# One encoder block on one core: the border to the down projection, the adaLN sums, and who forms the lower parts of the heads' weights

## The reference, cut to what matters

```
mod = silu(c) @ w_ada + b_ada                      # 6 vectors of 2048: shift, scale, gate, twice
h = rmsnorm(x, g_norm1) * (1 + sc1) + sh1
x = x + gt1 * hybrid_mixer(h)                      # mLSTM heads and windowed attention
h = rmsnorm(x, g_norm2) * (1 + sc2) + sh2
x = x + gt2 * ((silu(h @ w_gate) * (h @ w_up)) @ w_down)   # w_down: 5632 x 2048
out = rmsnorm(x, g_final)
```

## Time and profile before

| what | us |
|---|---|
| median of 3 executions (2424.16 to 2429.18) | 2427.79 |
| the profiled execution, its own time | 2428.71 |
| its span in the profile | 2426.9 |
| heads' stage, bodies 1 to 5 | about 231 to 733 |
| attention | about 737 to 838 |
| out projection, second norm | 838 to 1017 |
| gate and up projections | 1017 to 1901 |
| down projection and end | 1901 to 2427 |

### The profile page before, as it was taken

The page is one execution under the profiler, slowest core; times in us unless marked ns, Lnnn a source line. Parts: engine busy times, 40 slices in busy tenths (PEclk is TensorE's granted clock), DMA queues, the critical chain, the costliest instruction groups (busy, mean ns, idle before and its releaser), DMA issues.

```text
span 2426.9 us, 27227 instructions
## 1 busy us (share of the span) xinstructions
PE 2278.1 (94%) x10372; PEld 1888.2 (78%) x10372; DVE 1544.6 (64%) x1752; ACT 892.5 (37%) x1041; POOL 249.1 (10%) x89
## 2 busy tenths in 40 slices
PE   4898989899997899899999999999999799999997
PEld 4776868787885788788888888888888688888886
DVE  5667565656577557667877887788878434444443
ACT  4233222223235522354444444444444333333332
POOL 0000333333331111100000000000000000000000
PEclk7789989999998999899999999999999899999998
DMA  9843434353453168424444443444443654555452
GB/s 342 293 152 104 168 110 174 104 190 107 171 175 143 61 233 320 162 70 156 165 139 137 138 166 130 140 146 156 150 144 125 271 186 181 199 183 198 182 199 114
DMA packets 188065, 405.27 MB, mean 167 GB/s; under 512 B 9152, under 2 KB 67792, under 8 KB 172368
## 3 DMA queue, kind: packets, MB, share of 16 engines
q1 hardware_dynamic: 174960, 388.01, 45.1%
q10 hardware_dynamic: 13024, 16.13, 1.9%
HBM read 384.19 MB, written 19.92 MB: 167 GB/s over the span
## 4 chain that ended last, share of the span: by engine, by line
PE 78%; DVE 13%; issue 4%; ACT 2%; DMA 1%; SPq 1%; POOL 0%; DVEq 0%; ACTq 0%; POOLq 0%
PE ps L1712 23%; PE ps L1713 23%; PE ps L1714 23%; DVE acc L1051 2%; DVE qk L1254 2%; PE ps L1846 1%; PE ps L1767 1%; DVE acc L1284 1%; DVE qk L1251 1%; PE ps L2120 1%; PE ps L1859 1%; PE ps L1857 1%; PE ps L1961 1%; PE ps L1746 1%; DMA fr<-in_w_ada 1%
## 5 line engine op out<-in xcount | busy, mean ns | idle before, releaser
L885 ACT ACTIVATE whi<-wraw 128x1024 fp32r<-128x1024 f32 x200 | 212.1, 1061 | 261.6 <-PE ps L1714 137.2
L1712 PE MATMUL ps<-h_hi,whi 128*128 128x512 f32 x720 | 288.2, 400 | 13.9 <-DVE h_lo L1080 13.9
L1712 PE MATMUL ps<-d_hi,whi 128*128 128x512 f32 x704 | 276.7, 393 | 15.6 <-DVE d_lo L1656 8.3
L1545 DVE TENSOR_TENSOR wlo<-wraw,whi 128x1024 fp32r<-128x1024 f32 x200 | 240.8, 1221 | 76.9 <-ACT whi L885 76.9
L1713 PE MATMUL ps<-h_lo,whi 128*128 128x512 f32 x720 | 283.9, 394 | 0.0
L1714 PE MATMUL ps<-h_hi,wlo 128*128 128x512 f32 x720 | 283.3, 393 | 0.0
L1714 PE MATMUL ps<-d_hi,wlo 128*128 128x512 f32 x704 | 275.8, 392 | 0.0
L1713 PE MATMUL ps<-d_lo,whi 128*128 128x512 f32 x704 | 275.8, 392 | 0.0
L1654 DVE TENSOR_TENSOR wlo<-wraw,whi 128x2048 fp32r<-128x2048 f32 x44 | 100.8, 2291 | 267.0 <-ACT whi L950 267.0
L1712 PE MATMUL ps<-whi,sk_hi 128*128 128x512 f32 x640 | 251.8, 393 | 4.6 <-DVE u2b L1585 4.6
L1714 PE MATMUL ps<-whi,sk_lo 128*128 128x512 f32 x640 | 249.6, 390 | 0.0
(11 more groups left out here) (294 smaller groups left out, 3884.7 us busy)
## 6 DMA issues: line engine op xcount, KB each, us to landing
araw<-in_w_ada SPq DMA_DIRECT2D x64, 1024.0 KB, 5.7
wraw<-in_w_gate SPq DMA_DIRECT2D x88, 512.0 KB, 3.8
wraw<-in_w_up SPq DMA_DIRECT2D x88, 512.0 KB, 4.7
d_raw<-aT_keep SPq DMA_DIRECT2D x44, 1024.0 KB, 4.8
wraw<-in_w_down SPq DMA_DIRECT2D x44, 1024.0 KB, 7.1
wraw<-in_w_in SPq DMA_DIRECT2D x39, 1024.0 KB, 5.3
acc<-in_w_up SPq DMA_DIRECT2D x40, 512.0 KB, 5.5
fr<-in_w_ada SPq DMA_DIRECT2D x32, 512.0 KB, 7.2
```

Source lines behind the costliest of these rows:

```text
L885: A(EHI[e % 4], src, ACT.Copy).then_inc(uhi_ok, 1)
L1545: V_.tensor_tensor(ELO[e % 4], src, EHI[e % 4].bitcast(F32), ALU.subtract).then_inc(ulo_ok, 1)
L1712: pe.matmul(o, w_hi, m_hi, start=first, stop=False)
```

## The change

Three things. (1) At the border SP loads the activations of d = 0 as soon as their buffer is free and each block of weights as soon as its own buffer is; ACT copies activations first, weights second, each with its own wait; DVE follows in that order and makes `sum_low` between the two at d = 0. The buffers `d_hi`, `d_lo` of d = 0 and 1 trade places. (2) The eight late adaLN sums are finished by 16 matmuls with a column of ones (`ada_sums`) into 16 columns of one bank, and one DVE copy. In the bodies all 16 stand behind `slot(h, 6)`. (3) POOL's `lo` is gone; DVE forms the lower parts of pieces 13 to 46 in its own `body`, behind `weigh` and ahead of `layer_norm`, `mlstm_out` and `conv_pair`.

```diff
@@ buffers @@
-        d_hi = [... for i, o in enumerate((araw_off, big + 49152))]
-        d_lo = [... for i, o in enumerate((araw_off + 8192, big + 57344))]
+        d_hi = [... for i, o in enumerate((big + 49152, araw_off))]
+        d_lo = [... for i, o in enumerate((big + 57344, araw_off + 8192))]
@@ SP, down steps @@
-                if d < 2:
-                    sp.wait_ge(ulo_ok, 28 * NU)
-                    sp.wait_ge(u_used, 28 * NU - 12)
-                else:
+                if d == 0:
+                    sp.wait_ge(u_used, 28 * NU - 18)
+                elif d >= 2:
                     sp.wait_ge(dlo_ok, 2 * d - 2)
...
                 sp.dma_start(d_raw[d % 2][:], ...)
+                if d < 2:
+                    sp.wait_ge(ulo_ok, 28 * NU - 3 + 3 * d)
                 sp.dma_start(w3(wraw[d % 2], 4), w_down...)
@@ POOL, heads @@
-            def lo(s, par):
-                pool.wait_ge(whi_ok, s + 1)
-                pool.tensor_tensor(wlo[par][:], wraw[par][:], whi[par][:].bitcast(F32), ALU.subtract)...
-            pool.wait_ge(wlo_ok, 13)
             with pool.Fori(1, HEADS) as h:
-                body(h, True)
-            body(4, True)
-            body(5, False, steps=4)
+                norm(h)          # waits var_ok, then rs = ve ** -0.5
+            norm(4)
+            pool.wait_ge(wlo_ok, NB)
@@ ACT, down_hi @@
-                if d < 2:
-                    act.wait_ge(u_used, 28 * NU - 2 + 2 * d)
+                if d >= 2:
+                    act.wait_ge(d_used, 4 * d - 4)
                 else:
-                    act.wait_ge(d_used, 4 * d - 4)
+                    act.wait_ge(u_used, 28 * NU - 3 + 3 * d)
+                act.wait_ge(da_ld[d % 2], 16 * (d // 2 + 1))
+                A(d_hi[d % 2][:], d_raw[d % 2][:], ACT.Copy).then_inc(dhi_ok, 1)
                 act.wait_ge(dw_ld[d % 2], 16 * (d // 2 + 1))
+                if d == 0:
+                    act.wait_ge(u_used, 28 * NU - 2)
                 A(whi[d % 2][:], wraw[d % 2][:], ACT.Copy).then_inc(dhi_ok, 1)
-                act.wait_ge(da_ld[d % 2], 16 * (d // 2 + 1))
-                if d == 1:
-                    act.wait_ge(u_used, 28 * NU)
-                A(d_hi[d % 2][:], d_raw[d % 2][:], ACT.Copy).then_inc(dhi_ok, 1)
@@ DVE @@
             def ada_take(n, which, bank):
-                dve.wait_ge(ada_sum, n + 1)
-                j = 4 * (n % 4)
-                V_.tensor_reduce(modp[:, which, j:j + 4], ps[bank][:]...)
+                dve.wait_ge(ada_sum, n)
+                V_.tensor_copy(modp[:, which, :], ps[bank][:, 0:KT]).then_inc(modp_ok, 1)
+            def lower(s, par):
+                dve.wait_ge(whi_ok, s + 1)
+                V_.tensor_tensor(wlo[par][:], wraw[par][:], whi[par][:].bitcast(F32), ALU.subtract)...
@@ DVE, body, step j @@
                     if mixing and j < 4:
                         weigh(m, j)
+                    if not isinstance(h, int) or 5 + 8 * h + j < NB:
+                        lower(5 + 8 * h + j, (1 + j) % 2)
                     if mixing and j == 5:
                         layer_norm(m)
...
-                    if kind != "end" and j in (6, 7):
-                        ada_part(h, kind, j)
+                    if kind != "end" and j == 7:
+                        ada_take(h, h + 1, 6)
@@ DVE, down_lo @@
                 dve.wait_ge(dhi_ok, 2 * d + 1)
-                V_.tensor_tensor(wlo..., wraw..., whi..., ALU.subtract).then_inc(dlo_ok, 1)
-                dve.wait_ge(dhi_ok, 2 * d + 2)
                 V_.tensor_tensor(d_lo..., d_raw..., d_hi..., ALU.subtract).then_inc(dlo_ok, 1)
+                if d == 0:
+                    sum_low(NCH)
+                dve.wait_ge(dhi_ok, 2 * d + 2)
+                V_.tensor_tensor(wlo..., wraw..., whi..., ALU.subtract).then_inc(dlo_ok, 1)
@@ DVE, before down step 1 @@
-                    sum_low(NCH)
                     sum_high(NCH)
@@ PE @@
-            def ada_turn(hidx, banks, j0=0):
...
-                        last = pe.transpose(ps[bank][:, i * P:(i + 1) * P], acc[:, j * P:(j + 1) * P], ident[:])
+            def ada_sums(hidx, bank):
+                pe.wait_ge(ada_acc, hidx * 8 + 8)
+                for j in range(KT):
+                    last = pe.matmul(ps[bank][:, j:j + 1], acc[:, j * P:(j + 1) * P], ones[:, 0:1], start=True, stop=True)
+                last.then_inc(ada_sum, 1)
@@ PE, body @@
                     if j == 6:
-                        ada_turn(h + 6, (6, 7))
+                        ada_sums(h + 6, 6)
                     if j == 7:
-                        pe.wait_ge(modp_ok, h * 4 + 2)
-                        ada_turn(h + 6, (6, 7), 2)
                         turn_v(h, mixing)
```

More of the change, by code:

```diff
@@ L223, in program @@
         d_raw = [at(f"d_raw{i}", [P, TB, S], F32, big + i * 8192) for i in range(2)]
[L224 to L225 removed]
+        d_hi = [at(f"d_hi{i}", [P, TB, S], F32R, o) for i, o in enumerate((big + 49152, araw_off))]
+        d_lo = [at(f"d_lo{i}", [P, TB, S], F32R, o) for i, o in enumerate((big + 57344, araw_off + 8192))]
         xr = at("xr", [P, KT, S], F32, big + 16384)
@@ L499, in _, with norm @@
                 pool.tensor_tensor(rsx[:, tb:tb + 1], rsx[:, tb:tb + 1], halfneg[:, 0:1], ALU.pow).then_inc(rsx_ok, 1)
-            def lo(s, par):
-                pool.wait_ge(whi_ok, s + 1)
[L503 to L512, removed]
-            pool.wait_ge(wlo_ok, 13)
+            def norm(h):
+                pool.wait_ge(var_ok, h)
+                pool.tensor_tensor(rs, ve, halfneg, ALU.pow).then_inc(rs_ok, 1)
             with pool.Fori(1, HEADS) as h:
-                body(h, True)
-            body(4, True)
-            body(5, False, steps=4)
+                norm(h)
+            norm(4)
+            pool.wait_ge(wlo_ok, NB)
             def vlo(v):
@@ L1058, in front_lo @@
                                  whi[s % 2][:, 0:width].bitcast(F32), ALU.subtract).then_inc(wlo_ok, 1)
+            def lower(s, par):
+                dve.wait_ge(whi_ok, s + 1)
+                V_.tensor_tensor(wlo[par][:], wraw[par][:], whi[par][:].bitcast(F32), ALU.subtract).then_inc(wlo_ok, 1)
             def modulation(quarter):
@@ L1285, in ada_b @@
                                             op0=ALU.mult, op1=ALU.add).then_inc(ada_acc, 1)
-            def ada_part(h, kind, j):
-                which = h + 1
-                for b in range(2):
-                    dve.wait_ge(ada_sum, h * 4 + (2 * (j - 6) + b - 3))
-                    q = 4 * (2 * (j - 6) + b)
-                    V_.tensor_reduce(modp[:, bass.ds(which, 1), q:q + 4].rearrange("p a k -> p (a k)"),
-                                     ps[6 + b][:].rearrange("p (a b) -> p a b", a=4), AX.X, ALU.add)\
-                        .then_inc(modp_ok, 1)
             def conv_pair(h, t):
@@ L1407, in _ @@
                 elif u == 3:
-                    for b in range(4):
-                        ada_take(16 + b, 2 + 6, 4 + b)
+                    ada_take(5, 2 + 6, 6)
                 elif u == 4:
-                    dve.wait_ge(modp_ok, 24)
+                    dve.wait_ge(modp_ok, 9)
                     add_bias(2)
@@ L1440, in _ @@
                 if v == 7:
-                    for b in range(4):
-                        ada_take(20 + b, 3 + 6, 4 + b)
+                    ada_take(6, 3 + 6, 4)
                 if v == 11:
-                    for b in range(4):
-                        ada_take(24 + b, 4 + 6, b)
+                    ada_take(7, 4 + 6, 0)
                 for n in range(4, 24):
@@ L1481, in _ @@
             join_squares(2, KT, done=True)
-            for b in range(3):
-                ada_take(28 + b, 5 + 6, 4 + b)
             def mean_squares(k):
@@ L1490, in _ @@
             mean_squares(1)
[L1491 removed]
+            ada_take(8, 5 + 6, 4)
             dve.wait_ge(n_rs, 1)
@@ L1737, in x_block @@
                     last.then_inc(xT_ps, 1)
-            def ada_turn(hidx, banks, j0=0):
-                if j0 == 0:
-                    pe.wait_ge(ada_acc, hidx * 8 + 8)
-                for b, bank in enumerate(banks):
-                    for i in range(4):
-                        j = 4 * (j0 + b) + i
-                        last = pe.transpose(ps[bank][:, i * P:(i + 1) * P], acc[:, j * P:(j + 1) * P], ident[:])
-                    last.then_inc(ada_sum, 1)
+            def ada_sums(hidx, bank):
[3 more added lines that the diff above has]
+                last.then_inc(ada_sum, 1)
             def ada_columns(quarter):
```

28 lines of the change are left out of this document (13 added, 15 removed).

## The result

| | median us | runs | profiled execution | its span |
|---|---|---|---|---|
| before | 2427.42 | 7 (2422.32 to 2429.18) | 2428.71 | 2426.9 |
| after | 2435.75 | 7 (2432.81 to 2438.74) | 2436.83 | 2435.0 |

The ratio is 1.0039, with a 95% interval of 1.0028 to 1.0050: the change makes the kernel 8.3 us slower by the medians. That lies in the predicted range (2423.5 to 2437.5), 5.25 us above the predicted 2430.5.

What follows compares the result with a forecast made beforehand. PE, busy 94% of the span, was taken as the bound. Terms -10.0 - 0.5 - 0.3 + 0.5 + 13.65 + 5.1 - 2.8 - 0.8 - 2.3 = +2.55 us gave 2430.4, rounded 2430.5; range 2423.5 to 2437.5.

Steps and rivals of the forecast that it cites:

- rival 2: Clock stays low longer behind each new wait, deciding from 2.5 us per wait: 2436 us; chance 0.32.
- the late sums outside the heads: Sums finished by columns of ones: -0.5 behind the second norm, -0.3 in attention; no gain for PE itself.
- Border: Between last unit and down projection: the 7.3 us wait and 2.7 us of slow clock go, -10.0 (bounds -10.2, -7).
- the 8.3 us of step 1: Down projection, step 1: PE's wait for DVE's lower part was to stay at 8.3 us.
- Ahead of head 1 and its slots: 7.1 us wait shrinks to 2.7, fresh 3.2 wait: +0.5; then head 1's slots +13.65, plus clock +5.1.
- The clock's 1.7 for a wait: Head 1: 1.7 us lost to low clock behind each of three new waits, +5.1 (bounds 0 and 2.8 each).
- the three steps with their clock: Head 1, slots 3, 4 and 5 start late waiting for DVE's lower part: +13.65, and +5.1 for the clock.
- Rest of head 1: From the end of slot 5: 9.5 us wait goes, one of 5 to 6 for `turn_v` comes; -2.8 (-4 to -1).
- The price of undoing it: Without the new waits on `wlo` in head 1 the change would be 19 us faster.
- Heads 2 and 3: 6.15 us waits replaced by `turn_v` waits of 5 to 6 us: -0.4 a head, -0.8 in all (-3 to +2).
- Columns against transposes: Late adaLN sums: 16 columns of ones take 1.95 us, 16 transposes 1.91; PE gains nothing, +-0.1 for each of eight.
- the sum's two terms for it: Columns of ones: -0.5 behind the second norm's sum and -0.3 in attention, from saved DVE reductions.

Runs made afterwards that it cites:

- e1_border: Only the border edit, put on the kernel before: 2415.15 us, -11.2 against before, ratio 0.9956.
- e4_no_columns: The changed kernel without the columns of ones (border edit and DVE's lower parts only): 2434.62 us, +8.3 against before, ratio 1.0037.
- e10_three: The changed kernel with DVE's lower part moved ahead of diag, combine and weigh in body 1, steps 1 to 3 only: 2413.66 us, -11.5 against before.
- e5_early: The changed kernel with DVE's lower part moved ahead of diag, combine and weigh in all steps of body 1: 2407.70 us, -17.4 against before.
- e2_columns: Only the eight late sums by columns of ones, put on the kernel before, POOL keeping the lower parts: 2425.40 us, -1.0 against before, ratio 0.9996.
- e6_wide: The changed kernel with each late-sum matmul streaming 128 columns of ones instead of one: 2434.18 us, +9.1 against before, ratio 1.0034.
- e12_vt_wide: e7_mixed with ACT evacuating v columns ahead of the sigmoids and 128-wide columns of ones in bodies 1 to 4: 2384.29 us, -40.8 against before.
- e7_mixed: e5_early with the four last sums by transposes into four banks again, bodies 1 to 4 keeping columns of ones: 2403.82 us, -21.3 against before.

## Why the prediction came out as it did

The number lies in the range and 5.25 above the forecast. It fell where rival 2 stood (2436), but not by rival 2's cause: of the three slots behind a wait of 4.3 us only one lost more than 2.5 us to the clock. (Rival 2's own sum takes 1 us for half of the way from -0.8 to +3 in heads 2 and 3; it is 1.9, and the rival stands at 2437.) The outcome "slower" had 0.35, "same" 0.50. That the total came so near is in part luck: the late sums outside the heads cost 12.4 us more than their terms, and in the traces heads 1 to 3 gave 5.3 more than theirs (1.4 and 3.9), mostly by the same columns.

- **Border: right.** -10.0 predicted, -10.1 in the traces of the changed kernel and of e1_border; -11.2 by the medians of e1_border. The 0.3 us to spare and the 8.3 us of step 1 are in the trace.
- **Ahead of head 1 and its slots: right.** The wait of 7.1 us is 2.7, the fresh one 3.2. Slot 2 starts 0.7 earlier (+0.5 predicted, bounds -3 and +2), a number good to some 4 us only: in e4_no_columns, the same code up to there, it starts at 242.53 and not at 246.36. Slot 6 starts at 330.78 for 305.5, +25.3, where the terms give 0.5 + 13.65 + 5.1 + the fresh wait of 5.5 = +24.75. The clock's 1.7 for a wait measured 1.7 to 3.0. Taken alone (e10_three), the three steps with their clock were worth 19.8 for 18.75.
- **Rest of head 1: the size right, the reason wrong.** From slot 6 to the next `spread_m` PE gained 10.2 (8.3 by the terms). The wait of 5 to 6 us for `turn_v` did not come, 0.4 did: the last wait on `wlo` and a longer sum had used it up (e5_early, without that wait on `wlo`, has 4.9).
- **The price of undoing it: too low.** "No such waits in head 1 ... alone would make the change 19 us faster" measured 25.7 (e5_early). The 19 was the three steps and their clock, and these measured 19.8. It left out steps 0 and 4, worth 5.9 together (e10_three), most of it step 0's wait of 3.2 with its clock. That the wait of slot 6 delays nothing beyond the chain to `turn_v` was nearly right: 1.1 of 5.3 counts.
- **Heads 2 and 3: mis-sized**, -4.7 for -0.8. The prediction let waits of 5 to 6 us take the place of 6.15 us; 1.8 and less came. The columns and not the lower parts did this: without them heads 2 and 3 lose 2.8 (e4_no_columns), and with POOL's lower parts they still gain 6.6 (e2_columns).
- **Columns against transposes: the failed step.** "16 columns of ones take 1.95 us, 16 transposes 1.91" took a row of 8 columns for one of 16. The true price is 3.63, and another 0 to 3.4 behind it through the clock, which no term held. It cost 12.4 us against the terms outside the heads. What heads and columns did to each other hid most of it: the part alone is -1.0, against the -0.8 of the sum's two terms for it.
- **The Trainium skill.** Beside that row the prediction cited TensorE: Matmul & The Clock Gate, LDWEIGHTS, and found that the trace agrees that the load of 128 columns sets the time. e6_wide shows it cleanly (128 streamed columns in 3.7 us, one column in 3.6); what the row did not show was that there are two loads for each matmul. The same page of the Trainium skill has under its clock gate that idle time lowers the clock. The waits of head 1 agree (0.73 to 0.85), but here it also fell where PE had no idle time at all.

## What to carry to other kernels

When a row's count is used as a price, check it against the loop that it comes from: x16 may be 8 matmuls of two instructions each. When an instruction is moved into another engine's list, compare its place with the order in which its inputs arrive in every instance of the body, the one peeled instance too; moving `lower` up by three calls in one of five bodies was worth 26 us. A cost that lies ahead of a wait shows nothing until the wait is gone, so an edit that brought 0 (e6_wide) deserves a second look once its cover is removed (e12_vt_wide, 6 us).

## What the runs showed of the hardware that I had not expected

- A float32 matmul with a column of ones is two weight loads and two matmuls in the trace (256 for 128), 3.63 us for 16. A float32 transpose of the same block is one of each (16 in 1.91 us).
- Streaming 128 columns instead of one leaves the sum's time the same (3.7 and 3.6 us).
- The granted clock falls behind such a sum although PE is busy without a gap, to a mean of 0.71 to 0.74 over the next 6 us in most traces, and stays at 1.00 behind the 128-wide one. It doesn't do the same each time: behind body 4's sum it was at 1.2 GHz for 6.8 us in e7_mixed, about half of that in the kernel after, and not at all in e5_early. Why stays open.
- POOL's hold on DVE is visible in the convolutions: with `lo` on POOL the longest step took 5.16 us, with POOL idle none of the 64 took more than 0.754. The row is of the kernel after:

```profile
L1249 DVE SCALAR_TENSOR_TENSOR qk<-convin,cols,qk x64: 750/752/754, 171.4 to 587.1; 128x512 f32<-128x512 f32 x64
```
